# The retention heads' gate tiles as 2x2 blocks with seven products

## The reference

```python
h = rmsnorm(x, p['norm_pre_mix']) * (1 + sc1) + sh1
q, k, v, g, xr, gr = jnp.split(h @ p['w_in'], SPLITS, axis=-1)
o, s_new = retention(q, k, v, s_ret.astype(f32))             # q, k after rope; 4 heads
ret_y = groupnorm(o) * p['ret_gn_w'] * jax.nn.silu(g)
branch_ret = ret_y @ p['w_br_ret']
branch_rnn = (rg_lru(causal_conv(xr)) * gelu(gr)) @ p['w_br_rnn']
ga, gb = jnp.split(jax.nn.sigmoid(h @ p['w_mgate'] + p['b_mgate']), 2, axis=-1)
mixed = (ga * branch_ret + gb * branch_rnn) @ p['w_out']
x = x + g1 * rmsnorm(mixed, p['norm_post_mix'])
h2 = rmsnorm(x, p['norm_pre_ffn']) * (1 + sc2) + sh2
fg, fu = jnp.split(h2 @ p['w_ffn_in'], 2, axis=-1)
x = x + g2 * rmsnorm((jax.nn.silu(fg) * fu) @ p['w_ffn_out'], p['norm_post_ffn'])
```

## Time and profile before

| | us |
|---|---|
| median of 3 runs | 1374.01 (1373.72 to 1374.78) |
| profiled execution | 1375.0 |
| its span | 1373.2 |
| TensorE busy in the span | 1336.7 |
| one head's period (1 to 3) | 131.0 |

### The profile page before, as it was taken

The page is one execution under the profiler, slowest core; times in us unless marked ns, Lnnn a source line. Parts: engine busy times, 40 slices in busy tenths (PEclk is TensorE's granted clock), DMA queues, the critical chain, the costliest instruction groups (busy, mean ns, idle before and its releaser), DMA issues.

```text
span 1373.2 us, 24780 instructions
## 1 busy us (share of the span) xinstructions
PE 1336.7 (97%) x10380; PEld 1263.0 (92%) x10380; DVE 815.3 (59%) x1159; ACT 569.0 (41%) x847; POOL 206.9 (15%) x324
## 2 busy tenths in 40 slices
PE   6999999999999999999999999999899999999997
PEld 3899999988998898899889898999899999999996
DVE  4559888622353594268437734784787888853223
ACT  4667778211222321232224223426555666543221
POOL 1122232000114122301320131000011121100001
PEclk8999999999999999999999999999999999999998
DMA  9412122583424434524442353227054766743323
GB/s 371 172 62 93 63 77 78 207 334 126 178 77 161 154 109 150 178 90 144 148 159 72 137 181 126 78 78 265 2 165 123 183 165 173 181 126 102 95 85 66
DMA packets 61630, 189.91 MB, mean 138 GB/s; under 512 B 6608, under 2 KB 10192, under 8 KB 61136
## 3 DMA queue, kind: packets, MB, share of 16 engines
q1 hardware_dynamic: 44880, 141.80, 29.9%
q0 software_dynamic: 15488, 44.44, 12.5%
q10 hardware_dynamic: 1152, 2.10, 0.4%
HBM read 164.76 MB, written 23.55 MB: 137 GB/s over the span
## 4 chain that ended last, share of the span: by engine, by line
PE 77%; issue 7%; DVE 7%; DMA 4%; ACT 3%; SPq 1%; POOL 1%; DVEq 0%; ACTq 0%; POOLq 0%
PE ps L935 49%; PE ps L1360 14%; PE ps L944 5%; PE ps L1200 2%; DMA out_rs<-state 1%; PE ps L987 1%; PE ps L1183 1%; DMA ada_raw<-in_w_ada 1%; PE ps L1212 1%; PE ps L1244 1%; PE ps L1230 1%; PE ps L1086 1%; DMA raw<-in_w_out 1%; SPq L846 1%; DVE w_lo L1879 1%
## 5 line engine op out<-in xcount | busy, mean ns | idle before, releaser
L935 PE MATMUL ps<-h_hi,w_hi 128*128 128x272 f32 x1520 | 322.1, 293 | 4.5 <-DVE w_lo L1879 3.7
L935 PE MATMUL ps<-h_hi,w_lo 128*128 128x272 f32 x1520 | 315.3, 289 | 0.0
L935 PE MATMUL ps<-h_lo,w_hi 128*128 128x272 f32 x1520 | 314.5, 288 | 0.0
L1879 DVE TENSOR_TENSOR w_lo<-raw,w_hi 128x1024 fp32r<-128x1024 f32 (+2 forms) x154 | 183.9, 1198 | 190.3 <-ACT w_hi L1445 188.6
L935 PEld LDWEIGHTS ps<-h_hi,w_hi 128*128 128x128 f32 x1520 | 241.0, 189 | 16.3 <-issue 9.0
L1445 ACT ACTIVATE w_hi<-raw 128x1024 fp32r<-128x1024 f32 (+2 forms) x154 | 157.6, 1024 | 216.8 <-PE ps L935 116.9
L935 PEld LDWEIGHTS ps<-h_lo,w_hi 128*128 128x128 f32 x1520 | 239.7, 189 | 0.0
L935 PEld LDWEIGHTS ps<-h_hi,w_lo 128*128 128x128 f32 x1520 | 238.4, 190 | 0.0
L2175 DVE SCALAR_TENSOR_TENSOR state<-state,ps 128x512 f32<-128x512 f32 x64 | 41.0, 682 | 97.5 <-PE ps L1244 97.3
L935 PE MATMUL ps<-a_hi,w_hi 128*128 128x272 f32 x308 | 64.0, 289 | 0.2 <-DVE w_lo L1879 0.2
L2592 POOL DMA_DIRECT2D s_raw<-in_w_fin x18 | 15.6, 865 | 321.7 <-DMA s_raw<-in_w_fin 321.7
(11 more groups left out here) (311 smaller groups left out, 2762.3 us busy)
## 6 DMA issues: line engine op xcount, KB each, us to landing
raw<-in_w_head SPq DMA_DIRECT2D x48, 512.0 KB, 3.9
state<-in_state POOLq DMA_DIRECT2D x32, 512.0 KB, 4.6
out_rs<-state POOLq DMA_DIRECT2D x32, 512.0 KB, 4.4
raw<-in_w_rnn SPq DMA_DIRECT2D x24, 512.0 KB, 3.5
ada_more<-in_w_ada SPq DMA_DIRECT2D x23, 512.0 KB, 7.8
raw<-in_w_fin SPq DMA_DIRECT2D x20, 512.0 KB, 5.4
s_raw<-in_w_fin SPq DMA_DIRECT2D x36, 256.0 KB, 5.6
s_raw<-in_w_fin POOLq DMA_DIRECT2D x36, 256.0 KB, 4.9
```

What stands on the lines that cost most here:

```text
L935: mm = nc.tensor.matmul(dst[:, half, :], a, b[:, half * HALF:(half + 1) * HALF], start=first and j == 0, stop=last and j == 2)
L1879: V.tensor_tensor(lo[:, 0:cols], raw_slab(i)[0][:, 0:cols], hi[:, 0:cols].bitcast(F32), ALU.subtract).then_inc(lo_ready, 1)
```

## The change

The four gate tiles of a head become two pairs. A pair's weights, 256 channels by 1024 rows, are four blocks of 128 x 512: A = (A11, A12) for the upper tile, A21 and A22 for the lower one; the input's blocks are B11, B12, B21, B22, by halves of rows and of tokens. Seven products of 12 matmuls replace 96 matmuls; they accumulate into three banks q, s and t. The sums of input blocks (XC, XB, XA, XD) are made once, in head 0, from the unsplit input, which is saved to DRAM after the normalisation and loaded back (`h_again`). The weight sums: S1 and S3 by accumulating transfers of GpSimd into `s_head` (`add_blocks`), S2 and S4 in place by DVE. The split sums of the input take the places of `gbr` and `acc`. So `gbr` is saved to DRAM by ScalarE, and each branch tile is evacuated by ScalarE to one of four places (two in `vf`, two in `cosin`) and written or added to DRAM by GpSimd (`add_branch`); both come back before the mix. The cosines are loaded anew for each head. The diff, cut:

```diff
+HEAD_PRODUCTS = (("q", "A", 0, "B11"), ("t", "s13", 0, "XC"), ("q", "s24", 0, "XA"), ("s", "A", 1, "B21"),
+                 ("q", "s13", 1, "XB"), ("t", "s24", 1, "B22"), ("q", "a22", 0, "XD"))
-    return tiles + [("g", e) for e in range(ET)]
+    return tiles + [("pair", i) for i in range(ET // 2)]
...
     SP
+            def load_blocks_of_pair(kind, h, i):
+                below = w["w_head"][h, 8 + 2 * i + 1]
+                if kind == "s13":
+                    if (h, i) != (0, 0):
+                        last = pl.kinds["s24"][pair_number(h, i) - 1]
+                        sp.wait_ge(lo_ready, last + 1)
+                    for s in range(2):
+                        sp.dma_start(s_head[:, s, :], below[:, 0:BLOCK]).then_inc(s_head_in, 16)
...
+            sp.dma_start(kept_h, x_in[:]).then_inc(h_saved, 16)
...
-            sp.dma_start(cosin[:], w["cosin"]).then_inc(cosin_in, 16)
+            sp.wait_ge(h_saved, again(1))
+            for part in range(2):
+                ks = slice(part * KD // 2, (part + 1) * KD // 2)
+                sp.dma_start(h_again[:, ks, :], kept_h[:, ks, :]).then_inc(h_back, 16)
+                load_to(pl.slab[("v", 0, 2 + part, "w", 0)])
             for h in range(H):
+                load_to(pl.slab[("v", h, ET - 1, "w", 0)])
+                if h:
+                    wait_product(sp, h - 1, 1, PRODUCTS)
+                sp.dma_start(cosin[:], w["cosin"]).then_inc(cosin_in, 16)
...
     TensorE
+            def gate_pair_of_head(h, i, after):
+                for side in range(2):
+                    claim(("pair", h, i, side))
+                slabs, number, used = pair_slabs(h, i), pair_number(h, i), set()
+                for n, (bank, name, side, x) in enumerate(HEAD_PRODUCTS):
+                    pe.wait_ge(lo_ready, pl.slab[slabs[name]] + 1)
+                    if n in (2, 4, 5, 6):
+                        pe.wait_ge(gate_copied, 4 * number + {2: 1, 4: 3, 5: 3, 6: 4}[n])
...
+                    if n == 3:
+                        for u in after[("g", 2 * i)]:
+                            unit(h, u)
+                for u in after[("g", 2 * i + 1)]:
+                    unit(h, u)
...
     ScalarE
+                if m:
+                    save_branch(m - 1)
...
+            def send(h, m):
+                uses = KD // SENT * h + m // SENT
+                if uses:
+                    act.wait_ge(acc_added[m % SENT], 16 * uses)
+                evacuate(("br", h, m), sent(m))
+
+            def all_sent(h):
+                for i in range(SENT):
+                    act.wait_ge(acc_added[i], 16 * (KD // SENT) * h)
...
+            def gate_pair_of_head(h, i, after):
+                first, number = first_of_pair(h, i), pair_number(h, i)
+                split_to(first + 2)
+                if i == 0:
+                    act.wait_ge(q_ready, h + 1)
+                    if h:
+                        all_sent(h)
+                split_to(first + 3)
+                copy_head(h, i, 0, 1, "q")
+                copy_head(h, i, 1, 2, "t")
+                copy_head(h, i, 2, 3, "q")
+                for u in after[("g", 2 * i)]:
+                    unit(h, u)
+                split_to(first + 4)
+                copy_head(h, i, 3, 5, "q")
...
+                split_to(first + 5)
+                for u in after[("g", 2 * i + 1)]:
+                    unit(h, u)
...
     DVE
+            def gate_pair_of_head(h, i, after):
+                first, number = first_of_pair(h, i), pair_number(h, i)
+                split_to(first + 1)
+                s2, s4, upper = s_head[:, 0, :], s_head[:, 1, :], raw_slab(first)[0]
+                dve.wait_ge(lo_ready, first + 2)
+                do(V.tensor_tensor(s2, s2, upper[:, 0:BLOCK], ALU.add))
+                do(V.tensor_tensor(s4, s2, upper[:, BLOCK:2 * BLOCK], ALU.add), sums_ready)
+                split_to(first + 3)
...
     GpSimd
+                    if h:
+                        for m in {1: (0, 1, 2, 3), 2: (4, 5), 3: (6, 7)}.get(b, ()):
+                            add_branch(h - 1, m)
+                        if b == 1:
+                            add_blocks(h, 0)
                     if u:
                         store_state(u - 1)
+                    if b == (4 if h else 1):
+                        add_blocks(h, 1)
             store_state(H * NB - 1)
+            wait_product(pool, H - 1, 1, PRODUCTS)
...
+            pool.dma_start(gbr[:], kept_gbr).then_inc(back_in, 16)
+            pool.dma_start(acc[:], kept_acc).then_inc(back_in, 16)
```

More of the change, by code:

```diff
@@ L102, in __init__ @@
         self.ringed = []
+        self.product_end = {}
         self.half_tile = {}
@@ L118, in add_slab @@
         mine.append(len(self.slabs))
-        if kind != "early":
+        if kind not in ("early", "a22"):
             self.ringed.append(len(self.slabs))
@@ L309, in make_plan, with pair @@
                     block(b)
+    def pair(h, i, after):
+        slabs = pair_slabs(h, i)
+        for name, key in slabs.items():
+            pl.add_slab(key, BLOCK if name == "a22" else COLS)
+        for side in range(2):
+            pl.add_tile(("pair", h, i, side))
+        for n, (_, name, _, _) in enumerate(HEAD_PRODUCTS):
+            pl.step(slabs[name])
+            pl.product_end[(h, i, n + 1)] = pl.steps
+        for part in range(2):
+            for u in after[("g", 2 * i + part)]:
+                unit(h, u)
     for h in range(H):
@@ L312, in make_plan @@
         for name, i in head_tiles(h):
-            if name == "br":
+            if name == "pair":
+                pair(h, i, after)
+            elif name == "br":
                 br_tile(h - 1, i)
@@ L403, in hybrid_layer_kernel @@
         ps = top.enter_context(nc.psum_tensor("ps", [P, 8, 512], F32))
+        kept_h, kept_gbr, kept_acc = (nc.dram_tensor(f"kept_{name}", (P, KD, T), F32, kind="Internal").ap()
+                                      for name in ("h", "gbr", "acc"))
         h_scope = ExitStack()
@@ L1289, in _ @@
                 for name, i in head_tiles(h):
-                    if name == "br":
+                    if name == "pair":
+                        gate_pair_of_head(h, i, after)
+                    elif name == "br":
                         branch(h - 1, i)
@@ L1564, in _, with save_branch @@
                         roots(roots_at(NR))
+            def save_branch(m):
+                act.wait_ge(*took(("bn", m)))
+                act.dma_start(kept_gbr[:, m, :], gbr[:, m, :]).then_inc(gbr_saved, 16)
             for m in range(KD):
@@ L1601, in unit, with ahead_in_branch @@
+            def ahead_in_branch(h, m):
+                split_to(pl.slab[("br", h, m // 2, "w")] + (1 if m == KD - 2 else AHEAD))
             def unit(h, name):
@@ L1653, in _ @@
                 for name, i in head_tiles(h):
-                    if name == "br":
-                        split_to(pl.slab[("br", h - 1, i // 2, "w")] + AHEAD)
+                    if name == "pair":
+                        gate_pair_of_head(h, i, after)
+                    elif name == "br":
+                        if i < KD - 1:
+                            ahead_in_branch(h - 1, i)
+                        send(h - 1, i)
+                        if i == KD - 1:
+                            ahead_in_branch(h - 1, i)
                     else:
@@ L2100, in branch @@
             def branch(h, m):
-                key = ("br", h, m)
-                split_to(pl.slab[("br", h, m // 2, "w")] + AHEAD)
-                wait_tile(dve, key)
-                if h == 0:
-                    do(V.tensor_copy(halves(acc[:, m, :]), out_tile(key)), *took(key))
-                    return
-                do(V.tensor_tensor(halves(acc[:, m, :]), halves(acc[:, m, :]), out_tile(key), ALU.add), *took(key))
+                split_to(pl.slab[("br", h, m // 2, "w")] + (1 if m == KD - 2 else AHEAD))
```

219 lines of the change are left out of this document (186 added, 33 removed).

## The result

The changed kernel takes 1430.3 us (1429.6 to 1432.3), the kernel before 1373.9 beside it: a ratio of 1.0411, 95% interval 1.0398 to 1.0424. The prediction was 1395.4, in a range of 1384 to 1414. So the direction was right and the size was not: +56.4 us where +21.4 was forecast.

What follows compares the result with a forecast made beforehand. TensorE, busy 1336.7 of 1373.2 us, bounds the kernel, so new waits count in full. -12.0 + 10.0 + 3 x (4.5 + 2.2) + 1.0 + 2.3 = +21.4 on 1374.0 gives 1395.4 us, range 1384 to 1414.

Steps and rivals of the forecast that it cites:

- The products: Gate tiles of all heads: 96 fewer matmuls at 0.125 us each, a gain of 12.0 us, 3.0 a head.
- The chain of sums: Before a pair's third product: TensorE waits for update, S2 and S4, high and low part; 2.2 us, bounds 1.9 to 2.6.
- The first pairs: Heads 1 to 3: third product waits for ScalarE's copy, held until all branch tiles land; 4.5 us each, bounds 2.2 to 8.
- Head 0: Four stalls of TensorE in the first head's gate pairs, together 10.0 us.
- Claim: Head 0, first pair: it needs the banks of both tiles before it, q1's freed by DVE's rope; 1.75 us.
- third product: Head 0, first pair: waits until DVE finishes rope and sample values, then sums, high and low part; 4.1 us.
- second pair: Head 0, pair 1: the usual wait for the sums before the third product, 2.2 us.
- b1's bank: Head 0: ScalarE waits for `add_blocks(0, 1)`, queued behind state 0's store, and frees TensorE's bank late; 2.0 us, bounds 0 to 3.
- Moved transfers: Saved input ahead of gb0's weights and input halves between slabs at the retention's start: 1.0 us together, bounds 0 to 6.
- lie in idle time: The sums' four DVE operations a head and 1.5 slabs' more split per pair were taken to cost nothing.
- The clock: Matmuls at half clock behind a stall: one fall counted, 2.3 us, bounds 0 and 4 falls (9 us).
- Rival C: Branch transfers land late and the clock falls each time: +38 us, 1412 us; chance 0.18.

Runs made afterwards that it cites:

- f3: Changed kernel with six reorderings: sums earlier, ScalarE's wait split, b7's update before the split, GpSimd's accumulations and branch additions earlier, head 0 repaired; 1372.2 us, ratio 0.9985.
- g_order: Changed kernel, but GpSimd issues the additions of branch tiles 4 to 7 before it waits for the state's store; 1421.4 us, ratio 1.0333.
- d_b7: Changed kernel, but at the second pair DVE takes b6, the outputs and b7 before it splits the next slab; 1413.3 us, ratio 1.0286.
- c_fill: Changed kernel with no wait removed: extra matmuls on columns nobody reads, placed where TensorE would wait; 1416.7 us, ratio 1.0305.
- h_pair1: f3 with one edit taken back: sums of each head's second pair made after its first product again; 1381.9 us, ratio 1.0044.
- f2: Changed kernel with five reorderings, those of f3 without its last one, the repair in head 0; 1373.6 us, ratio 0.9993.

## Why the prediction missed

**The products: right in kind, 12.0 for 10.0.** 96 matmuls went. A head without new waits is 2.6 us shorter (f3), not 3.0. The term was too large because a product in the heads takes 1.54 us (672 matmuls in 86.4 us in f3, waits taken off) and not the 1.50 of the up-projection's rows: most take 1.49 to 1.52, but in four of the eight pairs the second and third take 1.67 and 1.61, and in six the fifth takes 1.61. Why these do is not shown.

**The chain of sums: right.** 2.2 forecast, 2.34 to 2.38 measured in all four second pairs, from the very rows named.

**The first pairs: right mechanism, right sum.** 3 x 4.5 = 13.5 forecast, 2.79 + 5.72 + 5.87 = 14.4 measured. That the sum came out is partly luck: head 1 landed earlier and the two that accumulate later than the common value I took, so errors of -1.7, +1.2 and +1.4 us cancelled. g_order shows that GpSimd's order decides it, as argued.

**Head 0: right places, 10.0 for 11.8.** Claim 1.50 (1.75 forecast), third product 3.84 (4.1), second pair 2.34 (2.2), and b1's bank 4.10 (2.0, bounds 0 to 3): the two accumulating transfers took 5.6 and 6.7 us to land and not the 4.9 of the earlier trace rows. In the working, the third product was due at 405.0; by its own terms (400.5, 1.75 and 3.0) it is 405.2, which gives 3.9 us instead of 4.1.

**Moved transfers: right, and free.** 0 for the 1.0 taken at the two starts; no wait before the mix.

**b7: missed, 10.3 us.** 7.7 in heads 1 to 3, and 2.6 more in head 0 (3.82 for the 1.2 of the earlier trace rows). The prediction followed every wait that the diff adds and none that it moves: it said that the sums and the slabs' further split "lie in idle time" of DVE. They do, but the split also waits, for a ScalarE that had three Silus at once, and the update queued behind it has a deadline. d_b7 shows it.

**The clock: missed, 21.3 for 2.3.** This is more than half of the error, and the step that failed is "preceded by dense work; I count one fall". Stalls of 2.3 to 5.9 us took the clock down at eleven places; dense work ahead did not protect it, for head 2's first pair, which stood 5.72 us up to 715.36, had 96 us (from 613.3) without a wait of over 0.4 us before it, and ran at 0.50 from 716 to 720. The bound of 4 falls was an expectation and no bound: there were 13 stalls of over 2 us. The Trainium skill ("TensorE: Matmul & The Clock Gate", HAM oscillation) says that gaps between bursts bring the half rate back. I had set it aside because this kernel's stalls are single. The traces and c_fill side with the Trainium skill: each of the eleven falls came with such a gap, and with the gaps filled nine were gone.

The prediction also says that the trace of before agrees "in one place only". That is wrong: it shows the half clock early on too, behind a stall of 2.43 us that ends at 40.61, with the clock full from 36 to 40 us.

```profile
40.61 0.52 PE L935 MATMUL ps<-h_hi,w_hi 128*128 128x272 f32 x2 [2.43 <-DVE w_lo L1879]
```

```profile
42.00:44.00 2.00, 2.00 (x10) 2.00 (x10) 1.17 (x3) 1.83 (x3) 0.00 (x0) 0.50 0.59 217
```

So a stall of that length had been followed by the half clock before any change, with some 1.7 us lost from 40 to 46 us, and the number of falls in the forecast could have been set higher.

The sum of these: +1.8 (head 0), +0.5 (second pairs), +0.9 (first pairs), +10.3, +19.0, +2.0 (products), -1.0 (starts) = 33.5 us, of the 34.9 between 1395.4 and 1430.3. The other 1.4 comes from the sum being of the two profiled executions, whose spans differ by 54.6 us, where the medians differ by 56.4.

Rival C had the clock falling each time and came nearest, at 1412, with a price of 2.3 a fall for four falls; it too lacked b7.

## What to carry to other kernels

When TensorE is the bound at full clock, price a stall at its own length and add the clock behind it: here 0.5 us per us of waiting (21.3 on 43.4) once a stage has many, and about 0.3 with four short ones far apart (h_pair1, an estimate). The mean granted clock of the executions without a profile says whether the profiled one is typical. After a change of the grain in which results become complete (here two tiles at once instead of one by one), walk every engine's queue through the next deadlines, for work that is not in the diff too. And where the account of span, waits and clock leaves a gain in the rest, as the 10.0 us here, the change is worth ordering anew: six small moves of instructions turned +4.1% into -0.15%.

## What the hardware showed that was not expected

- The granted clock fell behind stalls of 2.4 us (0.57 over 598 to 602 us). It held behind others: 2.37 and 2.54 us in head 2 of the same execution (1.00 over 742 to 750 and 756 to 760 us), and one of 3.40 us in the profiled execution of f2 (1.00 over 340 to 450 us). So the length of one stall alone does not decide it.
- The granted clock over the whole kernel differs between executions of one kernel, and the time goes with it: f2's ten range from 0.991 at 1370.95 us to 0.987 at 1375.67.
- Transfers of about the same size landed at very different times after their issue, by what stood around them. In the changed kernel, medians: 256 KB accumulated into SBUF by GpSimd, 6.1 us for the gate blocks but 4.8 for the up-projection's; 256 KB loaded plainly by SP, 4.5 and 5.4 for the same two. So accumulating cost 1.6 us more in the heads and nothing in the up-projection. Into DRAM, 272 KB accumulated took 6.5 us and written plainly 4.7, each in the median of six; GpSimd's plain writes of 512 KB took 4.1. The Trainium skill ("DMA: Bandwidth & Descriptors", Anatomy of one DMA) has the fixed part dominated by the last write's receipt, with DRAM the slowest target; the two targets differ here by only 0.4 us (6.1 and 6.5), less than the same kind of transfer does between two stages.
